# State read-out by pairs of groups in the two row halves of the array; impulse products ordered real parts first

## The reference

```
bu = einsum('blgh,gph->blgp', u, b_bar)          # 32 groups, 16 channels, 64 complex states per group
h  = associative_scan(a*h + bu)                  # over the frames
y  = real(einsum('blgp,ghp->blgh', h, c)) + d*u  # the read-out: back to 16 channels per group
g  = gelu(y);  out = g * sigmoid(g @ w_glu)
```

## Time and profile before

| | us |
|---|---|
| median of three runs | 2974.7 |
| the profiled execution's own time | 2973.88 |
| its span, first to last instruction | 2972.1 |
| TensorE matmul busy | 2899.5 (98%) |
| TensorE weight load busy | 2833.2 (95%) |
| VectorE busy | 1551.7 (52%) |
| ScalarE busy | 773.6 (26%) |
| GpSimd busy | 756.4 (25%) |

### The profile page before, as it was taken

One profiled execution on the slowest core, in us unless ns is written; L12 is line 12 of the kernel. 1 busy time (PEld: TensorE's weight loads), 2 busy tenths in 40 slices (PEclk: granted clock), 3 DMA queues, 4 the chain that ended last, 5 costly groups with the idle time before them and its releaser, 6 DMA issues.

```text
span 2972.1 us, 44233 instructions
## 1 busy us (share of the span) xinstructions
PE 2899.5 (98%) x18009; PEld 2833.2 (95%) x18009; DVE 1551.7 (52%) x1769; ACT 773.6 (26%) x1261; POOL 756.4 (25%) x350
## 2 busy tenths in 40 slices
PE   8999999999999999999999999999999999999996
PEld 8986799998999999999999999999899999999996
DVE  8867455556544445444463333555554544445444
ACT  6217644234311111111141111432341111111112
POOL 0106225122322112112152212521242112112113
PEclk9989999999999999999999999999999999999998
DMA  9273432110111111111111111121011111111111
GB/s 315 103 162 142 138 94 71 43 47 25 50 43 42 49 42 42 49 42 43 49 44 43 50 43 42 57 65 43 29 43 43 50 42 42 49 42 42 49 42 67
DMA packets 69132, 187.41 MB, mean 63 GB/s; under 512 B 7328, under 2 KB 25120, under 8 KB 67760
## 3 DMA queue, kind: packets, MB, share of 16 engines
q1 hardware_dynamic: 48928, 156.89, 15.4%
q10 hardware_dynamic: 20112, 29.22, 3.5%
HBM read 167.49 MB, written 21.61 MB: 64 GB/s over the span
## 4 chain that ended last, share of the span: by engine, by line
PE 93%; DVE 4%; ACT 2%; issue 1%; DMA 0%; DVEq 0%; POOL 0%; ACTq 0%; POOLq 0%; SPq 0%
PE PS L981 29%; PE PS L982 29%; PE PS L983 29%; PE PS L1125 2%; PE PS L1182 1%; PE PS L1145 0%; PE PS L1173 0%; PE PS L1022 0%; PE PS L1325 0%; DVE HL L761 0%; DVE XQL L755 0%; DVE XQL L749 0%; DVE X L811 0%; PE PS L1208 0%; ACT HH L1947 0%
## 5 line engine op out<-in xcount | busy, mean ns | idle before, releaser
L981 PE MATMUL PS<-XH,WH 128*128 128x354 f32 x3456 | 1127.6, 326 | 3.5 <-DVE X L710 1.1
L983 PE MATMUL PS<-XH,WL 128*128 128x354 f32 x3456 | 1121.8, 325 | 0.0
L982 PE MATMUL PS<-XL,WH 128*128 128x354 f32 x3456 | 1121.7, 325 | 0.0
L1575 POOL TENSOR_TENSOR WL<-WR,WH 128x1024 fp32r<-128x1024 f32 x216 | 529.4, 2451 | 2003.7 <-ACT WH L1672 2003.6
L981 PEld LDWEIGHTS PS<-XH,WH 128*128 128x128 f32 x3456 | 651.6, 189 | 7.7 <-DVE LNV L609 1.6
L982 PEld LDWEIGHTS PS<-XL,WH 128*128 128x128 f32 x3456 | 653.8, 189 | 1.2
L983 PEld LDWEIGHTS PS<-XH,WL 128*128 128x128 f32 x3456 | 649.9, 188 | 0.0
L1672 ACT ACTIVATE WH<-WR 128x1024 fp32r<-128x1024 f32 x216 | 228.9, 1060 | 1396.1 <-PE PS L983 1380.9
L981 PE MATMUL PS<-HH,WH 128*128 128x354 f32 x1662 | 543.9, 327 | 3.5 <-DVE X L811 2.1
L982 PE MATMUL PS<-HL,WH 128*128 128x354 f32 x1662 | 539.2, 324 | 0.0
L983 PE MATMUL PS<-HH,WL 128*128 128x354 f32 x1662 | 537.1, 323 | 0.0
(11 more groups left out here) (326 smaller groups left out, 2767.1 us busy)
## 6 DMA issues: line engine op xcount, KB each, us to landing
WR<-in_w SPq DMA_DIRECT2D x224, 512.0 KB, 3.2
WK<-in_w SPq DMA_DIRECT2D x16, 512.0 KB, 4.8
XR<-in_x ACTq DMA_DIRECT2D x8, 531.0 KB, 7.0
X<-in_x SPq DMA_DIRECT2D x8, 531.0 KB, 7.1
out_y<-X SPq DMA_DIRECT2D x8, 531.0 KB, 3.1
WX<-in_w SPq DMA_DIRECT2D x8, 512.0 KB, 5.3
CM<-scratch_cm SPq DMA_DIRECT2D x2, 2048.0 KB, 9.9
scratch_uj<-UJ ACTq DMA_DIRECT2D x1, 2128.0 KB, 7.0
```

The source lines that it names most:

```text
L981: pe.matmul(out, h, rh, start=start, stop=False)
L982: pe.matmul(out, h, rl, start=False, stop=False)
L983: return pe.matmul(out, l, rh, start=False, stop=stop)
L1575: pool.tensor_tensor(WL[:, s, :], WR[:, s, :], WH[:, s, :].bitcast(F32), ALU.subtract).then_inc(w_lo, 1)
```

## The change

Two functions of PE's list are rewritten. `impulses` runs over all 16 real parts first and then over all 16 imaginary parts; only its first matmul has the start flag, and only its last one the stop flag. `read_out` takes a tile of two groups in place of a group: first the TM products of both groups on the whole array, into the banks of the two groups; then the product with HR for both groups, each with only the 64 rows of its own half (weights, states and array rows); then the same with HI. Its matmul count is unchanged, two of TM and four of CM for two groups. The callers take tiles, and the wait for a free bank is now one per tile, for the second of the two banks.

```diff
-                for t in range(16):
-                    o = PS[:, 6, 32 * t:32 * t + 32]
-                    pe.matmul(o, PR[:, t].rearrange("p i c -> p (i c)"), CRD[:, t, :], start=True, stop=False, skip_group_check=True)
-                    mm = pe.matmul(o, PI[:, t].rearrange("p i c -> p (i c)"), NCID[:, t, :], start=False, stop=True, skip_group_check=True)
+
+                for pw, cd in ((PR, CRD), (PI, NCID)):
+                    for t in range(16):
+                        mm = pe.matmul(PS[:, 6, 32 * t:32 * t + 32], pw[:, t].rearrange("p i c -> p (i c)"), cd[:, t, :],
+                                       start=pw is PR and t == 0, stop=pw is PI and t == 15, skip_group_check=True)
                 mm.then_inc(par_kr, 1)
...
-            def read_out(g):
-                t, o = g // 2, PS[:, g % 8, 0:CC]
-                pe.matmul(o, TM[:, g, :], UG[:, g, :], start=True, stop=False)
-                pe.matmul(o, CM[0][:, g, :], HR[:, t, 0:CC], start=False, stop=False)
-                pe.matmul(o, CM[1][:, g, :], HI[:, t, 0:CC], start=False, stop=True).then_inc(ssm_y, 1)
+            def read_out(t):
+
+                for q in range(2):
+                    pe.matmul(PS[:, (2 * t + q) % 8, 0:CC], TM[:, 2 * t + q, :], UG[:, 2 * t + q, :], start=True, stop=False, skip_group_check=True)
+                for cm, h in zip(CM, (HR, HI)):
+                    for q in range(2):
+                        r = slice(64 * q, 64 * q + 64)
+                        mm = pe.matmul(PS[:, (2 * t + q) % 8, 0:CC], cm[r, 2 * t + q, :], h[r, t, 0:CC], start=False, stop=h is HI, skip_group_check=True)
+                        if h is HI:
+                            mm.then_inc(ssm_y, 1)
...
-                    for g in range(4):
-                        read_out(g)
+                    for t in range(2):
+                        read_out(t)
...
-            for g in range(4, 32):
-                if g >= 8:
-                    pe.wait_ge(ssm_act, g - 7)
-                read_out(g)
+            for t in range(2, 16):
+                if t >= 4:
+                    pe.wait_ge(ssm_act, 2 * t - 6)
+                read_out(t)
```

## The result

The changed kernel takes 2982.28 us (median of 14 runs, 2975.34 to 2989.09). The kernel before, in the same sessions, takes 2975.01 us (14 runs, 2973.37 to 2977.32). The ratio is 1.0026 [1.0018, 1.0033]: slower by 7.3 us. That is clear of noise; whether it is past the 0.2% that was taken as the bound is not, since 0.2% lies inside the interval. The forecast was 2973.9 us, and the range that was to hold the time ended at 2982.

What follows compares the result with a forecast made beforehand. PE was taken to bound the kernel (93% of the chain). Read-out -1.0 us, last copy +0.17 and impulse products 0 gave -0.8 us: 2974.7 - 0.8 = 2973.9 us, own range 2971 to 2977, 0.80 range 2968 to 2982.

Steps and rivals of the forecast that it cites:

- the sum: Read-out: a tile takes 1.29 us in place of 1.36, 1.0 us less over the 14 tiles behind `YB`.
- The first tile and a half run at 1.2 GHz as before: Read-out's start: 0.1 to 0.5 us less per tile there, moving the total by 0.5 us at most.
- the 364.9 of the prediction: Start of the output projection on PE: forecast at about 364.9 where it was 365.71.
- the end of the slow stretch: Read-out: 2.4 GHz from 347 or 348 on; a rise 3 us later costs about 1.5 us.
- Impulse products: 64 passes reordered, same weights and columns: 0 us, with 0.3 us either way.
- The price of a change of mode: Read-out, two changes per tile between whole array and row halves: 0.19 us each, ends 0.10 and 0.25.
- a tile of 1.29 us: Read-out: 8 x 0.113 + 2 x 0.19 us per tile, in place of 1.36 us.
- rival 2: Clock stays at 1.2 GHz through the read-out: +11 to +16 us, 2988.3 us; chance 0.20.
- The tail: Read-out's end: both copies of the last tile fall due together, so PE's next product comes 0.17 us later.
- The net of -0.8 us: Whole change: -1.0 + 0.17 us, with -3.3 to +0.9 us at the ends of the price of a change.
- Rivals 1 and 3: Read-out: mode changes cost next to nothing, 2968.5 us, chance 0.08; row halves don't overlap, 2980.1 us, chance 0.09.
- the stretch from 238.4 to 336.6: Evidence against rival 2: PE kept 2.4 GHz through many changes and some waits, busy 95.8 of 98.2 us.

Runs made afterwards that it cites:

- e3: The changed kernel plus 13 products nobody reads, filling PE's waits ahead of the read-out: 2973.08 us, ratio 0.9989 to the kernel before.
- e4: The kernel before plus the same 13 products nobody reads in PE's waits ahead of the read-out: 2972.38 us, ratio 0.9989.
- e2: The kernel before with only the new order of the impulse products: 2975.59 us beside 2975.35, ratio 0.9999.
- e1: The kernel before with only the new read-out, impulse products in the old order: 2982.32 us (nine runs), ratio 1.0022.
- e7: The changed kernel with the whole read-out in row halves, TM too, two tiles at a time: 2969.20 us, ratio 0.9978 to the kernel before.
- e8: The kernel before plus one product of 64 rows and one column per group, between TM and CM[0]: 3010.93 us (one run; kernel before 2975.52).

## Why the prediction was wrong

The step that failed stands in the sum: "The first tile and a half run at 1.2 GHz as before". Ten and a half tiles did, and the output projection starts at 372.46, 7.6 us behind the 364.9 of the prediction. The prediction took the end of the slow stretch as a property of the place, to be shifted by some microseconds at most ("a rise that comes 3 us later than now costs about 1.5 us"); it is a property of what PE does meanwhile. The same gaps that the sum counted at 0.19 us each went with the slow clock for 25 us in the place of 3.4.

The account in numbers. At 2.4 GHz throughout, the changed one takes 18.89 us (e3) and the one before 19.67 us (e4). As they run they take 30.22 and 21.38 us, so the slow clock costs 11.33 us in place of 1.71 us, 9.62 us more. With the 0.78 us that the change wins, 9.62 - 0.78 = 8.84 us, which is 30.22 - 21.38 again, since these are differences of the same four lengths. An independent sum is that of the tiles: ten at 2.37 - 1.31 = 1.06 us too much and the eleventh (365.97 to 367.84) at 0.56 make 11.2 us for the 11.33.

Point by point:

- Impulse products, taken as 0: right. e2 measures 0 within 0.1%, and a pass still starts 0.11 us after the one before it: 32 passes of PR between the starts of these two rows, (165.56 - 162.07) / 32.

```profile
162.07 3.65 PE L1032 MATMUL PS<-CRD,PR 128*128 128x32 f32 x32
165.56 0.77 PE L1032 MATMUL PS<-NCID,PI 128*128 128x32 f32 x4
```

- The price of a change of mode, 0.19 us from the earlier trace rows, and a tile of 1.29 us: right at 2.4 GHz, where a tile takes 1.31 us. With 8 x 0.113 = 0.90 that leaves 0.20 us a change. At 1.2 GHz, 2.37 - 8 x 0.222 = 0.59 us, 0.30 us a change, inside the 0.19 to 0.38 that rival 2 was priced with. The Trainium skill, "TensorEngine Tiling (Array Packing)", Key Properties, states a drain at a change of mode, without a price; these 0.20 us agree with it.
- The tail, +0.17 us for the second copy of the last tile: right. PE's wait for ACT ahead of the output projection is 0.63 us in e3 and 0.46 us in e4.
- The net of -0.8 us: right where the clock is the same (-0.78 us), and invisible in the time.
- Rivals 1 and 3 fall with the tile of 1.31 us: changes are not free, and the halves do overlap.
- Rival 2 had the mechanism, with "The changed list has two gaps in each tile" and the tile of 2.15 to 2.53 us, but a chance of 0.20, and its price was that of all 14 tiles. Measured are ten and a half of 14, and 2982.3 us in place of 2988.3. Its upper cases do occur: 2989.09 us was the slowest run, 2975.34 the fastest. The clock is what spreads the runs: with two levels, a mean granted clock of 0.991 costs 0.009 x 2973.5 = 27 us of the fastest run's span, and 0.986 costs 0.014 x 2987.3 = 42 us of the slowest's, 15 us apart (3 us either way by the rounding) where the times are 13.75 us apart. That it is the read-out's clock, by a number of slow tiles that differs from run to run, is shown for two executions (ten and a half tiles here, eight and a half in e1) and argued for the rest.
- What was held against rival 2 was the stretch from 238.4 to 336.6, where PE kept 2.4 GHz through many changes. That row is true and was no evidence: it shows PE keeping a clock that it had, as e3 does, and the question was whether it gets one back.

The Trainium skill, "TensorE: Matmul & The Clock Gate", Part 1, says that sustained activity releases the slow clock. The rise at 348.24 in e7, out of passes without gaps, agrees. By that sentence alone the changed read-out could be read either way; its trace shows 25 us at 0.50 with PE's busy column at 24.96.

What stays open: why the clock did come back at 367.2 (in e1 at 364.6, in e8 at 396.5), when nothing in PE's list changed there. Nor are gaps all there is to a slow clock: in the impulse products, passes of 32 columns, PE stands at 0.50 while PE and PEld are busy for 10.20 of 10.20 us (the last line of the stretches of the profile after).

## What to carry to other kernels

Before small gaps are put into a stretch, look at the granted clock at which the engine enters it: gaps that cost 0.2 us each at 2.4 GHz cost 9.6 us in sum where PE arrives at 1.2 GHz and does not get back. Read the weight loads' share beside PE's, because the overlapping records of matmuls hide gaps of this size; the share shows the gaps and does not tell the clock (next section). A row that shows an engine keeping its clock tells nothing about getting it back; and where modes must alternate, batch them (two tiles together won 10.8 us over one) or leave the second mode out (e7).

## What was not expected of the hardware

Nearly the same share of gaps stood beside either clock: 19.4 us at 1.00 with the loads busy for 78% (e3), 25 us at 0.50 with them busy for 80% (the changed kernel). And a product of one column per group, 32 in all, made the kernel before 35 us slower (e8, one run).
